# The next expert block's rows are turned between a block's up products and the turn of its gated values

## The reference, cut to what matters

```python
def run_block(args):
    tok, e, wt = args
    xb = x_pad[tok]
    h = jax.nn.silu(xb @ w_e1[e]) * (xb @ w_e3[e])      # w_e1, w_e3: 1024 x 512
    return (h @ w_e2[e]) * wt[:, None].astype(xb.dtype)  # w_e2: 512 x 1024
...
y = jnp.zeros((NT + 1, D), x.dtype).at[slot_tok].add(yb.reshape(P, D).astype(x.dtype))
```

## Time and profile before

| what | us |
|---|---|
| median of 3 runs | 1378.83 |
| lowest and highest of them | 1378.38, 1384.01 |
| the profiled execution, whole | 1386.88 |
| its span, first to last instruction | 1385.1 |
| start of the first turn of rows in the expert stage | 864.41 |
| start of the last block's down products | 1349.18 |

### The profile page before, as it was taken

How to read it: one execution, slowest core, us unless ns; L and a number is a source line. 1 busy time by engine, 2 the same in 40 slices (tenths; PEclk the granted TensorE clock), 3 DMA queues, 4 the chain that set the end, 5 groups by cost and what they waited for, 6 DMA issues and landing times. The chain is left out here.

```text
span 1385.1 us, 20473 instructions
## 1 busy us (share of the span) xinstructions
PE 1117.5 (81%) x8244; PEld 862.0 (62%) x8244; DVE 404.5 (29%) x847; ACT 356.8 (26%) x732; POOL 324.2 (23%) x316
## 2 busy tenths in 40 slices
PE   3899599889998759999999551888888778887870
PEld 3899498879996748888897451444444444444440
DVE  4568523951111344442322136111110101000013
ACT  5457423442221744443331030000000000000000
POOL 3344359621112412221542101101010000010003
PEclk9999789988888969999999855999999999999995
DMA  6222526163314221114323751899999999999975
GB/s 115 77 62 77 177 64 167 35 176 90 107 48 130 84 78 47 47 47 141 98 86 95 334 204 47 314 409 416 409 419 417 421 421 420 418 413 416 415 325 201
DMA packets 151814, 293.17 MB, mean 212 GB/s; under 512 B 42512, under 2 KB 117872, under 8 KB 135360
## 3 DMA queue, kind: packets, MB, share of 16 engines
q1 hardware_dynamic: 94224, 247.95, 46.8%
q10 hardware_dynamic: 53712, 35.33, 8.9%
q0 software_dynamic: 3808, 8.92, 2.0%
HBM read 267.59 MB, written 28.51 MB: 214 GB/s over the span
## 5 line engine op out<-in xcount | busy, mean ns | idle before, releaser
L472 PE MATMUL bank<-xhi,cv_w_hi 128*128 128x272 f32 x848 | 264.2, 312 | 10.4 <-POOL cv_w_lo L458 8.9
L2401 PE MATMUL bank<-e_w,b_xT 128*64 128x256 f32 x2048 | 233.0, 384 | 36.0 <-DVE b_xT L2432 25.1
L458 POOL TENSOR_TENSOR cv_w_lo<-cv_w_raw,cv_w_hi 128x1024 fp32r<-128x1024 f32 (+1 forms) x69 | 159.4, 2311 | 427.5 <-ACT cv_w_hi L451 421.4
L472 PE MATMUL bank<-xhi,cv_w_lo 128*128 128x272 f32 x848 | 254.0, 300 | 0.0
L472 PE MATMUL bank<-xlo,cv_w_hi 128*128 128x272 f32 x848 | 253.8, 299 | 0.0
L2401 PEld LDWEIGHTS bank<-e_w,b_xT 128*64 128x64 f32 x2048 | 144.2, 138 | 114.7 <-DVE b_xT L2432 29.5
L472 PEld LDWEIGHTS bank<-xhi,cv_w_hi 128*128 128x128 f32 x848 | 169.5, 200 | 15.7 <-POOL cv_w_lo L458 9.5
L472 PEld LDWEIGHTS bank<-xlo,cv_w_hi 128*128 128x128 f32 x848 | 169.8, 200 | 1.1
L472 PEld LDWEIGHTS bank<-xhi,cv_w_lo 128*128 128x128 f32 x848 | 169.2, 199 | 0.0
L2413 PE MATMUL bank<-e_w,b_hiddenT 128*64 128x512 f32 x512 | 128.4, 647 | 30.0 <-DVE b_hiddenT L2439 19.9
L2413 PEld LDWEIGHTS bank<-e_w,b_hiddenT 128*64 128x64 f32 x512 | 41.0, 147 | 95.4 <-issue 70.8
(11 more groups left out here) (410 smaller groups left out, 1603.6 us busy)
## 6 DMA issues: line engine op xcount, KB each, us to landing
e_w<-in_w_e SPq DMA_DIRECT2D x96, 2048.0 KB, 41.5
cv_w_raw<-in_w_in ACTq DMA_DIRECT2D x33, 512.0 KB, 3.9
cv_w_raw<-in_w_in SPq DMA_DIRECT2D x19, 512.0 KB, 3.8
expert_rows<-b_y ACTq DMA_DIRECT2D x64, 128.0 KB, 8.7
expert_rows<-cv_zero SPq DMA_DIRECT2D x8, 512.0 KB, 6.9
cv_w_raw<-in_w_br_b ACTq DMA_DIRECT2D x8, 512.0 KB, 3.6
o_raw<-in_w_out SPq DMA_DIRECT2D x16, 256.0 KB, 4.0
g_values_gates<-g_z_stage ACTq DMA_DIRECT2D x12, 272.0 KB, 4.5
```

The costliest lines, as they stand in the source:

```text
L458: self.k.nc.gpsimd.tensor_tensor(self.wlo[:, s, 0:nk, :], self.raw[:, s, 0:nk, :], self.whi[:, c % OPS, 0:nk, :].bitcast(F32), ALU.subtract)\
L472: last = self.k.nc.tensor.matmul(self.bank(c, h)[:, 0:HALF], w, x[:, d, cols], start=(d == 0 and n == 0), stop=(d == nk - 1 and n == 2))
L2401: last = nc.tensor.matmul(k.bank[bank][sl[a], 0:FH], xT[:, d, :], w[slot][:, d, FH * a:FH * a + FH], start=(d == 0), stop=(d == KD - 1))
```

## The change

In `products`, the turn of the rows becomes a function of its own, `turn`. Block 0's rows are turned ahead of the loop. Then each block issues its up products, the turn of block b + 1's rows, and only then the turn of its own gated values and the down products. On DVE the copy of the turned rows, now `keep_turned`, moves likewise: it is issued for block b + 1 between block b's gate and the copy of its turned gated values. The last block leaves both out. The further blocks (not needed here) turn their own rows ahead of themselves.

```diff
-        def products(pe, b, slot, n, prev):
+        def turn(pe, b, slot, n):
+
             pe.wait_ge(gathered[slot], 16 * n + 16)
             wait(pe, copied, b)
-
             nc.tensor.matmul(k.bank[0][:, 0:64], xg[:, slot, 0:128], k.ident[0:64, 0:64], start=True, stop=True)
             for d in range(1, KD):
                 last = nc.tensor.transpose(k.bank[0][:, 64 * d:64 * d + 64], xg[:, slot, 128 * d:128 * d + 128],
                                            k.ident[0:64, 0:64])
             last.then_inc(turned, 1)
+
+        def products(pe, b, slot, n, prev, ahead=True):
             pe.wait_ge(copied, b + 1)
             wait(pe, hidden, b)
...
                 last.then_inc(made, 1)
+            if ahead:
+                turn(pe, b + 1, (slot + 1) % RING, n + (slot + 1) // RING)
             pe.wait_ge(hidden, b + 1)
...
-        def vector_part(v, b, slot, n, prev):
+        def keep_turned(v, b):
             v.wait_ge(turned, b + 1)
             wait(v, up, b)
             nc.vector.tensor_copy(xT[:].rearrange("p k s -> p (k s)"), k.bank[0][:]).then_inc(copied, 1)
+
+        def vector_part(v, b, slot, n, prev, ahead=True):
             v.wait_ge(silu, b + 1)
             v.wait_ge(up, b + 1)
             wait(v, hturned, b)
             nc.vector.tensor_tensor(hm[:], act[:], k.bank[2][:, 0:FH], ALU.mult).then_inc(hidden, 1)
+            if ahead:
+                keep_turned(v, b + 1)
             v.wait_ge(hturned, b + 1)
...
-        def run_blocks(eng, part):
+        def run_blocks(eng, part, first=lambda b, slot, n: None, last={}):
+
+            first(0, 0, 0)
```

More of the change, by code:

```diff
@@ L2456, in run_blocks @@
             for b in range(RING * STEPS, NE):
-                part(eng, b, b % RING, b // RING, b - RING)
+                part(eng, b, b % RING, b // RING, b - RING, **(last if b == NE - 1 else {}))
             n = eng.value_load(k.nmore[0:1, 0:1], min_val=0, max_val=MORE)
@@ L2460, in run_blocks @@
                 with eng.Fori(0, n) as j:
-                    part(eng, j + NE, RING - 1, j + STEPS, j + NE - 1)
+                    first(j + NE, RING - 1, j + STEPS)
+                    part(eng, j + NE, RING - 1, j + STEPS, j + NE - 1, **last)
             return n
@@ L2484, in _ @@
             def _(pe):
-                run_blocks(pe, products)
+                run_blocks(pe, products, first=lambda b, slot, n: turn(pe, b, slot, n), last={"ahead": False})
             @block.scalar
@@ L2496, in _ @@
             def _(v):
-                run_blocks(v, vector_part)
+                run_blocks(v, vector_part, first=lambda b, slot, n: keep_turned(v, b), last={"ahead": False})
 def combine(k):
```

## The result

The changed kernel is slower: 1390.0 us as a median of 12 runs against 1382.67 us of the kernel before in its 12 runs of the same series, a ratio of 1.0057 with a 95% interval of 1.0036 to 1.0079. The profiled execution took 1395.0 us, its span 1393.3 us.

A forecast was written before the change was run, and what follows sets the result against it. The weight stream on fully busy DMA engines was taken as the bound. Block 0's w2 release 0, rate -0.9 and last block's clock 0 sum to -0.9 us on 1378.83, rounded to 1378.0 us, range 1375 to 1384.

The forecast's parts named there:

- The frame: Expert stage: the weight stream, not PE, fixes the end; late blocks stay at 16.0 us, DMA share at 1.01.
- PE's chain: Early blocks: PE's own sequence per block shortens by 1.14 us, from 13.97 to 12.83 us.
- the early gain: Blocks before the first wait for weights: about 10 us gained, all given back later as waits for weights.
- the last block ran at full clock: Last block: taken as 0 cost; a lower clock in its w3 products would cost 3.3 us, in its down products 1.7.
- a sign of being wrong: Late blocks: the prediction would be wrong if their pace left 16 us.
- The step from the up to the down products: Each early block: from 1.60 to about 2.11 us, 0.51 later, as DVE copies the turned rows first.
- The saved step behind the down products: Between a block's down products and the next up products: 1.65 us removed.
- The first wait: PE first waits for weights in block 10 at about 1003 us, instead of block 13 at 1054.
- Gathers are no term: Row gathers: no cost, since they land 8.6 us after issue and are issued more than two blocks ahead of use.
- The rate term: Weight stream, 1003 to 1054 us: rate rises 1.7%, from 412 to 419 GB/s, gaining 0.9 us.
- The rivals: Late blocks: low clock makes PE the bound (5%), turn waits for rows (2%); PE bound after all, faster (4%).
- the slower outcome: Whole kernel slower by over 0.5%: chance 0.07, from the low-clock and late-rows cases.

The follow-up runs named there:

- b_gather_apart: Kernel before, each gather held until the block's products with w3 are through, nothing moved on PE or DVE: ratio 1.0056, stream 483.4 us.
- e_gather_beside: Changed kernel, each gather held until the block that last held its slot has copied its result out, so beside its stores: ratio 0.9981, stream 475.1 us.
- b_store_apart: Kernel before, each block's two stores held until the next block's products with w3 are done, gathers unmoved: ratio 1.0042, stream 482.1 us.
- e_store_beside: Changed kernel, each block's two stores held until the next block's turn of rows, beside the gather: ratio 1.0016, stream 477.9 us.
- e_gather_late: Changed kernel, each gather held until the block's products with w1 are through: ratio 1.0053, stream 482.3 us.

## Why the prediction was wrong

The frame held. PE's chain was not the bound, the early gain was given back as waits, and the stream's length set the end. The DMA share stayed at 1.01, the clock of the late stretch was 0.96, in the range I gave, and the last block ran at full clock. But the pace of the late blocks left 16 us (16.43), which I had named as a sign of being wrong, and it did so at an unchanged DMA share.

**The size of the miss.** The measured 1390.0 us are 12.0 above the forecast. Of these, 7.3 are the change itself and 0.9 the gain that I had forecast. The other 3.8 are the kernel before, whose median was 1378.83 us over the 3 runs that I started from and 1382.67 over 12. That part is luck, and without it the result would still lie above the range.

**PE's chain.** I had 12.83 us, it was 12.48. The step from the up to the down products took 1.91 us (877.90 to 879.81 in block 0), not 2.11, because DVE starts the second of two copies 0.61 us after the first though that one takes 0.69, and the turn of rows starts 0.07 us ahead of the up products' end. The saved step behind the down products was larger by the rest. The first wait came in block 8 at 976 us instead of block 10 at 1003. The shorter chain alone would have put it into block 9; block 8's w3, the 17th load, came after (975.99 - 874.66) / 17 = 5.96 us a load, where I had 5.67, and that is already the slower stream. The sizes of PE's chain didn't reach the end.

**The gathers: the step that failed.** "Gathers are no term", I wrote, because they land in time for their use. I had asked only whether somebody waits for them. On a stream that is the bound they are not only a thing to be waited for but a load, and I didn't ask what they run beside. The change says nothing of POOL, but `fetch` waits for `turned`, and the moved turn moved all 29 gathers from 1.2 us behind the stores to 4.4 us ahead of them. That is the whole loss: moving the gathers alone makes it (b_gather_apart, 1.0056), moving them back alone removes it (e_gather_beside, 0.9981), and the same is true of the stores, to within 2 us of the stream (b_store_apart, e_store_beside).

**The rate term had the wrong sign.** "The same bytes" was right and I took the time for them as given, with a gain of 0.9 us from the difference of 412 and 419 GB/s between early and late. It was a loss of 6.9 us. The 412 wasn't a matter of the queue's depth. From 876 to 979 us a load landed 20.4 us after its issue in the kernel before and 30.0 us in the changed one, so the changed kernel has the deeper queue, and it has the lower rate. With the gathers back beside the stores the deeper queue gives the rate of before. The window of 880 to 980 us (DMA share and GB/s are the last two numbers) in the kernel before, the changed one and e_gather_beside:

```profile
880.00:980.00 100.00, 1.00 1.01 411
880.00:980.00 100.00, 1.00 1.01 403
880.00:980.00 100.00, 1.00 1.01 410
```

In the early stretch more gathers and stores fall on each microsecond. Without gathers the same window has 425 GB/s in both kernels, and 428 late (1054 to 1300 us), so most of the step between early and late is the gathers' too.

**The rivals.** None of mine was the cause; the slower outcome had 7 in 100 and came by a mechanism that I hadn't named. The products with w3 took 5.01 to 5.36 us instead of 3.67 in nine of the 23 blocks from block 9 on, behind waits of 1.9 to 3.0 us; in block 23, for one, the granted clock was 0.50 from 1225 to 1227 us, the lower of the two levels. Other waits as long had no fall behind them (2.66 us in block 10). Each fall cost up to 1.7 us, the spare time of the block took it, and the last block wasn't hit. The Trainium skill, "TensorE: Matmul & The Clock Gate", section "HAM oscillation — how this bites in real kernels", describes a kernel that loses the clock at every wait for DMA between sets of matmuls. This trace agrees that such waits can cost the clock, but not that each does.

The Trainium skill, "DMA: Bandwidth & Descriptors", section "Issuing engines are not separate DMA queues", says that transfers issued by SP, ACT and POOL run on the same 16 engines and interleave. The table of packets agrees: w1's and w3's grew from 629 to 640 ns in e_gather_late, and w2's from 315 to 325 in the changed kernel, with the place of a gather that another engine issued. That sentence should have sent me to look at what POOL and ACT issue and when.

**What stays open.** Why a gather alone holds the engines back more than one beside stores wasn't settled. The traces show that weight packets take some 770 instead of 616 ns while a gather runs alone, and some 720 while it runs beside stores, for 16384 bytes. What in the gather does this (its 4096-byte rows, its queue on POOL, the partitions that it writes) no run here took apart. The runs show that the company of the stores decides; they don't show by what means.

## What to carry to other kernels

When a stream of transfers is the bound and fully busy, its length isn't fixed by its bytes: ask of each change which small transfers it moves, through the semaphores that let them go, and what they will run beside. Follow the waits of every engine for a moved signal, the ones that the diff doesn't mention above all. And look for the quantity that repeats from run to run, here the length of the stream to within about 1 us, before reading a difference out of whole times that scatter by 10.

## What the runs showed of the hardware that I had not expected

- A gather of some 34 rows of 4096 bytes into 64 partitions, under way for 2.5 us, lowered the rate of all 16 engines from 419 to 334 GB/s while it ran, and to 364 with the two stores beside it, at an unchanged busy share of 1.01. In all, a gather cost the stream 1.13 us alone and 0.86 us beside stores, where its own bytes at 419 GB/s are 0.33.
- The busy share of the DMA engines didn't tell a stream of 416 GB/s from one of 409; it was 1.01 in both.
- Without gathers the stream's 190.6 MB took 450.5 us, 423 GB/s, stores included. That is no less than the 419 of the stretches with neither in the kernel before, so without gathers the two stores of 128 KB a block cost about their bytes.
